# Conditioning sums on GpSimd: 72 whole tiles in twelve stretches in place of 144 half tiles in eight

## The reference, cut to what matters

```
cond = jax.nn.silu(c)
for l in range(2):
    mod = (cond @ mod_w[l] + mod_b[l]).reshape(B, 9, D)
    u = rms_norm(h, norm_w[l, 0]) * (1 + mod[1]) + mod[0]
    h = h + 0.5 * mod[2] * swiglu(u, ...)
    ...
```

## Time and profile before

| | us |
|---|---|
| median of three runs | 4962.53 (4962.01 to 4971.61) |
| the profiled execution's own time | 4961.05 |
| its span | 4959.3 |
| PE busy | 4058.9 (82%) |
| DVE busy | 1996.8 (40%) |
| ACT busy | 1528.4 (31%) |
| POOL busy | 1199.2 (24%) |

### The profile page before, as it was taken

One profiled execution on the slowest core, in us unless ns is written; L12 is line 12 of the kernel. 1 busy time (PEld: TensorE's weight loads), 2 busy tenths in 40 slices (PEclk: granted clock), 3 DMA queues, 4 the chain that ended last, 5 costly groups with the idle time before them and its releaser, 6 DMA issues.

```text
span 4959.3 us, 45454 instructions
## 1 busy us (share of the span) xinstructions
PE 4058.9 (82%) x17223; PEld 3073.9 (62%) x17223; DVE 1996.8 (40%) x2138; ACT 1528.4 (31%) x1898; POOL 1199.2 (24%) x800
## 2 busy tenths in 40 slices
PE   4987979889698887987897976677898977566989
PEld 3854868657586676765676744664386845564467
DVE  3534445325353354535444434213245432324144
ACT  3345424224342343436333311011143421102033
POOL 3610656205563055630450000100000000110000
PEclk9998989999898998999998977888998987778999
DMA  4633646336463265643563411011454522001444
GB/s 149 218 90 107 219 159 229 113 117 210 160 216 112 78 220 174 215 130 91 178 220 107 161 60 61 1 60 61 143 180 144 188 77 78 0 13 47 154 152 144
DMA packets 490210, 649.31 MB, mean 131 GB/s; under 512 B 13051, under 2 KB 390418, under 8 KB 490066
## 3 DMA queue, kind: packets, MB, share of 16 engines
q1 hardware_dynamic: 466832, 568.50, 34.5%
q0 software_dynamic: 20736, 75.51, 4.6%
q10 hardware_dynamic: 2498, 3.39, 0.2%
HBM read 646.29 MB, written 1.05 MB: 131 GB/s over the span
## 4 chain that ended last, share of the span: by engine, by line
issue 57%; POOLq 15%; PE 13%; POOL 8%; DVE 3%; DMA 2%; ACT 1%; DVEq 0%; SPq 0%
POOL lora_w L495 6%; POOLq L510 5%; POOLq L502 5%; POOLq L500 3%; PE bank L701 2%; POOLq L508 2%; PE bank L937 2%; PE bank L1037 1%; PE bank L708 1%; PE bank L710 1%; PE bank L709 1%; PE bank L1044 1%; PE bank L1046 1%; DMA gate<-in_mod_w 1%; DMA wproj<-in_w_in 1%
## 5 line engine op out<-in xcount | busy, mean ns | idle before, releaser
L708 PE MATMUL bank<-wproj_hi,x_lo 128*128 128x512 f32 x2112 | 848.9, 402 | 58.3 <-DVE x_lo L1612 51.2
L710 PE MATMUL bank<-wproj_hi,x_hi 128*128 128x512 f32 x2112 | 832.5, 394 | 0.0
L709 PE MATMUL bank<-wproj_lo,x_hi 128*128 128x512 f32 x2112 | 832.1, 394 | 0.0
L701 PE MATMUL bank<-wproj,xT 128*128 128x384 f32 (+2 forms) x1984 | 769.2, 548 | 23.9 <-DMA wproj<-in_w_in 11.0
L1554 DVE TENSOR_TENSOR wproj_lo<-wproj,wproj_hi 128x4096 fp32r<-128x4096 f32 x132 | 615.9, 4666 | 324.3 <-ACT wproj_hi L1187 324.3
L701 PEld LDWEIGHTS bank<-wproj,xT 128*128 128x128 f32 x1984 | 381.9, 196 | 395.9 <-issue 256.8
L708 PEld LDWEIGHTS bank<-wproj_hi,x_lo 128*128 128x128 f32 x2112 | 403.0, 191 | 151.9 <-DVE x_lo L1612 56.0
L1187 ACT CAST wproj_hi<-wproj 128x4096 fp32r<-128x4096 f32 x132 | 480.1, 3637 | 20.7 <-DMA wproj<-in_ffn_w_gate_up 15.3
L710 PEld LDWEIGHTS bank<-wproj_hi,x_hi 128*128 128x128 f32 x2112 | 402.0, 190 | 87.3
L709 PEld LDWEIGHTS bank<-wproj_lo,x_hi 128*128 128x128 f32 x2112 | 403.5, 191 | 80.1
L471 POOL TENSOR_SCALAR rstd<-sumsq 128x2 f32<-128x2 f32 x21 | 4.0, 191 | 1804.5 <-ACT tok L1182 1766.5
(11 more groups left out here) (359 smaller groups left out, 5184.6 us busy)
## 6 DMA issues: line engine op xcount, KB each, us to landing
wproj<-in_ffn_w_gate_up SPq DMA_DIRECT2D x176, 1024.0 KB, 7.6
wdown<-in_ffn_w_down SPq DMA_DIRECT2D x132, 1024.0 KB, 5.6
wproj<-in_w_in SPq DMA_DIRECT2D x52, 1024.0 KB, 6.2
wproj<-in_ffn_w_gate SPq DMA_DIRECT2D x44, 1024.0 KB, 5.3
wproj<-in_ffn_w_up SPq DMA_DIRECT2D x44, 1024.0 KB, 7.8
gate<-in_mod_w POOLq DMA_DIRECT2D x72, 512.0 KB, 4.0
oT<-in_mod_w POOLq DMA_DIRECT2D x72, 512.0 KB, 5.2
wproj<-in_sb_w_qkv SPq DMA_DIRECT2D x48, 512.0 KB, 5.5
```

The costliest lines, as they stand in the source:

```text
L701: last = nc.tensor.matmul(proj_ps[t][:, 0:rhs.shape[2]], lhsT[:, c, t * P:(t + 1) * P], rhs[:, c, :], start=(c == 0), stop=(c == kc - 1))
L708: nc.tensor.matmul(ps, rounded(a_lo), rounded(b), start=first, stop=False, skip_group_check=True)
L709: nc.tensor.matmul(ps, rounded(a), rounded(b_lo), start=False, stop=False, skip_group_check=True)
L710: return nc.tensor.matmul(ps, rounded(a), rounded(b), start=False, stop=final, skip_group_check=True)
```

## The change

The same product is cut otherwise. A tile is now whole: all 8 row chunks of 256 columns, 1 MB, 72 of them, in twelve parts of six. GpSimd multiplies 2048 elements a partition by `cond` in place, adds halves three times (1024, 512 and 256 elements), the last into `mod_acc`, and then issues the fetch of the tile after the next, whichever part that belongs to; the first two fetches are issued before the first norm. Parts run in the first FFN, in the attention (from the attention's `rstd` on; in MLA from its inner `rstd` on) and in the second FFN of each layer. `mod_sums` and `mod_take` stand three times a layer, with 24 matmuls each. The buffers lie in other places: one over `oT2` and `gate`, one in `modrow`, the sums in `lora_w`'s place.

```diff
         gate = sb("gate", [P, NT, 512])
         lora_w = sb("lora_w", [P, 3, W_B])
         lvl = sb("lvl", [P, len(LEVELS), P])
-        mod_tile = [gate[:].rearrange("p a (b n) -> p (a b) n", n=256), oT[2][:]]
-        mod_prod = lora_w[:].rearrange("p a n -> p (a n)")[:, 0:1024].rearrange("p (c n) -> p c n", c=4)
-        mod_acc = modrow[:].rearrange("p a n -> p (a n)")[:, 0:MOD_COLS * P]
+        mod_tile = [mod_zone[:, 0:2 * D].rearrange("p (c n) -> p c n", c=KC),
+                    modrow[:].rearrange("p a n -> p (a n)")[:, 0:2 * D].rearrange("p (c n) -> p c n", c=KC)]
+        mod_acc = mod_zone[:, 2 * D:2 * D + MOD_COLS * P]
         prod_mask = sb("prod_mask", [P, 2, 2, P])
         headsum = sb("headsum", [P, P])
         restart = sb("restart", [P, SEQ])
...
 
             def mod_load(k):
 
-                layer, rest = divmod(k, MOD_ROWS)
-                block, half = divmod(rest, 2)
+                layer, block = divmod(k, MOD_TILES * MOD_PARTS // DEPTH_2)
                 if k >= 2:
                     pool.wait_ge(mod_read, k - 1)
                 src = A["mod_w_2"][layer].rearrange("(c p) n -> p c n", p=P)
-                nc.gpsimd.dma_start(mod_tile[k % 2], src[:, 4 * half:4 * half + 4, block * 256:(block + 1) * 256]
+                nc.gpsimd.dma_start(mod_tile[k % 2], src[:, :, block * 256:(block + 1) * 256]
                                     ).then_inc(mod_in[k % 2], DMA)
 
             def mod_part(i):
 
                 first, last = i * MOD_TILES, (i + 1) * MOD_TILES
-                mod_load(first)
-                mod_load(first + 1)
-                if i:
-                    pool.wait_ge(mod_summed, i)
                 for k in range(first, last):
-                    half = k % 2
+                    tile = mod_tile[k % 2]
                     pool.wait_ge(mod_in[k % 2], DMA * (k // 2 + 1))
-                    nc.gpsimd.tensor_tensor(mod_prod, mod_tile[k % 2],
-                                            cond[:, 4 * half:4 * half + 4].unsqueeze(2).broadcast_to([P, 4, 256]),
-                                            ALU.mult).then_inc(mod_read, 1)
-                    if k + 2 < last:
+                    nc.gpsimd.tensor_tensor(tile, tile, cond[:, :].unsqueeze(2).broadcast_to([P, KC, 256]), ALU.mult)
+                    pool.drain()
+                    nc.gpsimd.tensor_tensor(tile[:, 0:4], tile[:, 0:4], tile[:, 4:8], ALU.add)
+                    pool.drain()
+                    nc.gpsimd.tensor_tensor(tile[:, 0:2], tile[:, 0:2], tile[:, 2:4], ALU.add)
+                    pool.drain()
+                    if k == first and i:
+                        pool.wait_ge(mod_summed, i)
+                    at = (k - first) * 256
+                    nc.gpsimd.tensor_tensor(mod_acc[:, at:at + 256], tile[:, 0], tile[:, 1],
+                                            ALU.add).then_inc(mod_read, 1)
+                    if k + 2 < MOD_TILES * MOD_PARTS:
                         mod_load(k + 2)
-                    pool.drain()
-                    nc.gpsimd.tensor_tensor(mod_prod[:, 0:2], mod_prod[:, 0:2], mod_prod[:, 2:4], ALU.add)
-                    pool.drain()
-                    acc = mod_acc[:, (k - first) // 2 * 256:(k - first) // 2 * 256 + 256]
-                    if half == 0:
-                        nc.gpsimd.tensor_tensor(acc, mod_prod[:, 0], mod_prod[:, 1], ALU.add)
-                    else:
-                        nc.gpsimd.tensor_tensor(mod_prod[:, 0], mod_prod[:, 0], mod_prod[:, 1], ALU.add)
-                        pool.drain()
-                        nc.gpsimd.tensor_tensor(acc, acc, mod_prod[:, 0], ALU.add)
-                    pool.drain()
+                pool.drain()
                 pool.sem_inc(mod_added, 1)
 
+            mod_load(0)
+            mod_load(1)
             for l in range(DEPTH):
                 inverse_rms((0, 2, D))
                 if l == 0:
                     pool.wait_ge(cond_ready, 1)
-                mod_part(2 * l)
+                mod_part(3 * l)
                 inverse_rms((0, 2, D))
                 if l % 3 == 2:
                     inverse_rms((0, 2, MLA_Q_RANK), (2, 4, MLA_KV_RANK))
+                mod_part(3 * l + 1)
                 inverse_rms((0, 2, D))
-                mod_part(2 * l + 1)
+                mod_part(3 * l + 2)
 
             def heads_rms(columns, width, eps):
                 pool.wait_ge(head_ss, n.diff + 1)
...
             for l in range(DEPTH):
                 norm()
                 ffn()
-                mod_sums(2 * l)
+                mod_sums(3 * l)
                 norm()
                 if l % 3 == 2:
                     mla()
                 else:
                     attend("sb" if l % 3 == 0 else "moba")
                     out_proj(KC)
+                mod_sums(3 * l + 1)
                 norm()
                 ffn()
-                mod_sums(2 * l + 1)
+                mod_sums(3 * l + 2)
             n.scaled += 2
             for l in range(DEPTH_2):
                 n.small += SMALL_DMAS * DMA
...
             for l in range(DEPTH_2):
                 act.wait_ge(hid_ready, n.hidden)
                 if l == 0:
-                    act.wait_ge(mod_added, MOD_PARTS)
+                    act.wait_ge(mod_summed, MOD_PARTS)
                 for dst, src in ((lora_w[0:R_W, 0, :], A["rwkv_w2_2"][l]), (lora_w[R_W:P, 0, :], A["rwkv_a2_2"][l]),
                                  (lora_w[:, 1, :], A["rwkv_g2_2"][l, 0:P]), (lora_w[0:R_G - P, 2, :], A["rwkv_g2_2"][l, P:R_G])):
                     act.dma_start(dst, src).then_inc(small_in, DMA)
...
                 else:
                     attend("sb" if l % 3 == 0 else "moba")
                     out_proj(KC)
+                mod_take(3 * l + 1)
                 ffn(gained(3 * l + 2))
-                mod_take(2 * l + 1)
+                mod_take(3 * l + 2)
             final_norm()
             for l in range(DEPTH_2):
                 modulation(l)
...
 CONST_DMAS = 5
 VEC_DMAS = 3 * DEPTH + 4 + DEPTH_2 * 15
 SMALL_DMAS = 4
-MOD_PARTS = 2 * DEPTH
-MOD_TILES = DEPTH_2 * N_MOD * D // 256 * 2 // MOD_PARTS
+MOD_PARTS = 3 * DEPTH
+MOD_TILES = DEPTH_2 * N_MOD * D // 256 // MOD_PARTS
 MOD_COLS = DEPTH_2 * MOD_ROWS // MOD_PARTS
 ROUND = 1.5 * 2.0 ** 23
 PI_DOWN = float(np.nextafter(np.float32(math.pi), np.float32(0)))
```

More of the change, by code:

```diff
@@ L279, in program @@
         modA = sb("modA", [P, 3, KC])
+        under = ExitStack()
+        mod_zone = under.enter_context(nc.sbuf_tensor("mod_zone", [P, 2 * D + 3 * W_B], F32))
+        under.close()
         oT.append(sb("oT2", [P, BC, SEQ]))
@@ L2180, in _ @@
                 ffn(gained(3 * l))
-                mod_take(2 * l)
+                mod_take(3 * l)
                 norm()
```

## The result

The changed kernel takes 4973.18 us (median of 20 runs, 4963.48 to 4982.54), the kernel before beside it 4960.66 (20 runs, 4952.06 to 4971.61): ratio 1.0024, 95% interval 1.0017 to 1.0031. It is slower by 12.5 us; I had forecast 18 us faster. The time lies in my range, the sign is wrong.

A forecast was written before the change was run, and what follows sets the result against it. TensorE bounds FFN insides, but idles 113.4 us in eight waits for GpSimd. Removing 132 us less 114 us of collisions nets 18 us: 4961.05 - 18 + 1.5 = 4945 us, range 4890 to 4990.

The forecast's parts named there:

- Waits of 132 us removed: Square to first product at eight places: no part late any more, 69 + 42 + 20 us, together 132 us saved.
- norms at 60 us: GpSimd collides with VectorE's scalings and splits: 47 us at FFN starts, 13 us at three attention starts.
- MLA's inner norm: Four short VectorE scalings with GpSimd's product and adds between them: 7 us added.
- M: GpSimd's product of 2048 elements for a tile, taken at 3.6 us, bounds 1.89 and 4.7.
- the turns at `rstd`: GpSimd starts its product once `rstd` is done, then alternates with VectorE; 6 us at each of eight FFN starts.
- all parts in time: Six tiles take 66 us, some 95 with collisions, within every stretch; the rival of a late part had 0.08.
- inside FFNs ... I cost at nothing: First product to next square in FFNs: TensorE is the bound, 195.0 us against 195.1, so 0 us added.
- The attention's 47 us: Collisions inside attentions: stick-breaking 28, MLA's pairs 13, MoBA 6 us; floor 0, ceiling 117.
- The clock: TensorE slow after idle stretches in stick-breaking: 2 us allowed; the slower case priced it at 8 us.
- The slower rival: Attention pays in full as VectorE's chains wait for GpSimd; decides over 65 us; 60 us slower, 5022; chance 0.20.
- A: GpSimd's first add in a tile, 1024 elements, taken at 2.35 us.
- B: GpSimd's second add in a tile, 512 elements, taken at 1.26 us.

The follow-up runs named there:

- The kernel without the work: Changed kernel with GpSimd's conditioning fetches, products and adds all left out, column sums and hand-overs kept: 4818.89 us, ratio 0.9713.
- the kernel with half the tiles: Changed kernel with the product and first two adds left out for three of six tiles in each attention part: 4914.19 us, ratio 0.9917.
- the kernel with pieces: Changed kernel with each tile's product in four instructions of 512 elements and its first add in two of 512: 4974.87 us, ratio 1.0025.

## Why the prediction was wrong

- *Waits of 132 us removed, norms at 60 us*: right. -71.9 us against -72, FFN starts 23.4 us (24 said), attention starts 15.3 (15 said), MLA's 9.5. MLA's inner norm was held 6.5 us (its last scaling ends 30.1 us behind the first product; 23.7 without the work): 7 said. M at 3.6 us, the turns at `rstd` and all parts in time came as written; no wait for GpSimd ahead of the sums is left.
- *"inside FFNs ... I cost at nothing"*: wrong by 6.4 us against before. My own row told against it: the 195.1 us "without products" had 2 us more of tail, so an FFN with products was already paying 2 us. The kernel without the work shows 193.4.
- *The attention's 47 us (54 with the MLA's norm)*: the step that failed. With the norm it was 72, in all four attentions more than said: 36 for 28, 25 for 20, 11.5 for 6. I had called it a term with no row beside it, with a floor of 0 and a ceiling of 117 (the addends give 116), and took the middle by counting waits of VectorE. What the count lacked: (1) In stick-breaking the first two chains took 21.7 us together, for which I had 23, but I let the holds end there; the third chain was late as well (10.0, 11.7 and 7.6 us long against 4.2). (2) In the MLA I had 3 us a pair over 4.5 pairs. Three steps were 8.8, 7.1 and 2.5 us longer, the later ones not at all: the second pair's nine operations took 8.9 us in place of 1.6. One of them, called during GpSimd's DMA issue with M right behind it, waited for both and took 4.50 us; my count of mean waits had no such case. (3) The clock: I gave it 2 us in stick-breaking and nothing in the MLA, where it was 4 to 5. How MoBA's 11.5 us divide stays open.
- *The slower rival* was the right mechanism ("VectorE's chains waiting for GpSimd's holds"). I put its point of decision at 65 us in the four attentions without the MLA's norm, 72 with it. It was 72.2: on the point. The sign was turned by that and by the 6.4 us in the FFNs and 1.1 at the first square, which had no term. Its full price of 117 was not paid. A term of 47 without a row, 18 us under the change of sign and with bounds of 0 and 117, hardly allowed a chance as low as 0.20 for it. That the time fell into my range, 28 us off the forecast, is the range's width and not the sum.
- *The Trainium skill's* lock for the whole instruction ("SBUF — State Buffer", section "SBUF: two separate sides") is what 309.65 and 319.60 show for the chains' operations with two SBUF inputs, which no row of before had shown.

The change is a loss since it trades late first products at eight places (132 us, 113 of them TensorE's waits for GpSimd) for holds on VectorE in all twelve stretches. With the attention parts taken out the same tiles are a gain of 1.5%, and with one tile in each step 2.7%.

## What to carry to other kernels

Work of GpSimd that shares memory with VectorE is not free beside it: here it cost most of its length where VectorE was last (4.5 to 4.8 us of a tile's 7.2 on the head chains, 5.6 at each FFN start), and nearly nothing where VectorE waited for another engine. Look for the idle stretches of VectorE inside the steady loop and release one unit of the side work into each, by VectorE's own counter; here a gate at the beginning only moved the hold to the next operation, and cutting the instructions only spread it. When a term of a forecast has no row and wide bounds, weigh the other sign by how few us of that term turn it.

## What the runs showed of the hardware

- A product of GpSimd holds VectorE from before its own start, if it comes right behind a DMA issue. Two rows of the kernel after, the same operation of VectorE called 0.14 us into an issue, once with M behind the issue and once with nothing:

```profile
1634.49 0.91 POOL L484 DMA_DIRECT2D modrow<-in_mod_w  x1 [0.29 <-POOL mod_zone L502]
1634.63 4.50 DVE L1647 TENSOR_TENSOR arena<-arena 128x64 f32<-128x64 f32 x1
1635.42 3.62 POOL L493 TENSOR_TENSOR mod_zone<-mod_zone,cond 128x2048 f32<-128x2048 f32 x1
...
1656.06 0.91 POOL L484 DMA_DIRECT2D modrow<-in_mod_w  x1 [0.29 <-POOL mod_zone L502]
1656.20 0.22 DVE L1647 TENSOR_TENSOR arena<-arena 128x64 f32<-128x64 f32 x1
```

  So the issue alone does not keep VectorE out (the chain operations at 312.88 and 316.07 in the kernel with half the tiles took their 0.69 us during issues too), but what VectorE calls during it may get in only behind M. In four traces all 21 short operations with two SBUF inputs that were called 0.2 to 0.8 us ahead of such an M were held. In the row at 538.77 the split is called 0.57 us ahead of M; it takes 8.48 us in place of 4.43 (542.96 + 4.4 = 547.3). The same at 319.60, and at 505.28 in the kernel with pieces, where four products of 1.0 us went ahead of it one behind another. This is read from timelines; no kernel tried it by itself.
- Nine tiles of 7.2 us (M, A, B) cost an FFN no more than six did (218.8 and 219.0 us). I read this as one slip: once it is paid, VectorE is no longer last. No kernel tried it by itself.
